# Merge stage of a hybrid encoder step: the mixed rows turned by VectorE instead of TensorE, two sets of product banks, the router one tile later

## The reference

```python
h = rmsnorm(x) * (1 + sc1) + sh1
o_hg, o_rw = hgrn2(h), rwkv7(h)                 # the two head groups: "mix", 1024 columns
x  = x + g1 * (concat(o_hg, o_rw) @ w_out)      # merge stage from here
h2 = rmsnorm(x) * (1 + sc2) + sh2
g_logits = h2 @ router_g_w + router_g_b         # 4 groups, top-1
e_logits = h2 @ router_e_w + router_e_b         # 8 experts in the group, top-2
gates = softmax(g_logits)[grp] * softmax(top2(e_logits))
x = x + g2 * sum(gates * expert(h2))            # 32 SwiGLU experts, then a final rmsnorm
```

## Time and profile before

| | us |
|---|---|
| median of 3 runs | 2940.0 (2937.04 to 2946.08) |
| the profiled execution's own time | 2939.38 |
| its span | 2937.6 |
| PE busy | 2701.2 (92%) |
| DVE busy | 1522.7 (52%) |
| ACT busy | 842.3 (29%) |
| merge products (L2184), first to last start | 1667.9 to 1954.9 |

### The profile page before, as it was taken

The page is one execution under the profiler, slowest core; times in us unless marked ns, Lnnn a source line. Parts: engine busy times, 40 slices in busy tenths (PEclk is TensorE's granted clock), DMA queues, the critical chain, the costliest instruction groups (busy, mean ns, idle before and its releaser), DMA issues. The chain is left out here.

```text
span 2937.6 us, 80216 instructions
## 1 busy us (share of the span) xinstructions
PE 2701.2 (92%) x33393; PEld 1697.0 (58%) x33394; DVE 1522.7 (52%) x3711; ACT 842.3 (29%) x1739; POOL 352.0 (12%) x477
## 2 busy tenths in 40 slices
PE   6998999999999979899998699976999999999978
PEld 2443445454454558778877455535666666666653
DVE  3554466665566647677777344454333333333328
ACT  2654334444344424444444222210000000000006
POOL 0000000000000001112113000001222222122223
PEclk8999999999999989999999799987999999999999
DMA  8433123223242396556652685572798578778758
GB/s 311 157 129 134 55 101 129 101 92 108 83 159 103 118 239 166 163 146 171 183 157 87 196 311 205 208 272 103 274 367 319 226 273 325 276 293 314 301 206 345
DMA packets 307724, 580.30 MB, mean 198 GB/s; under 512 B 56494, under 2 KB 240742, under 8 KB 292168
## 3 DMA queue, kind: packets, MB, share of 16 engines
q1 hardware_dynamic: 257544, 486.12, 46.8%
q0 software_dynamic: 18736, 70.27, 6.9%
q10 hardware_dynamic: 31248, 21.08, 2.4%
HBM read 411.77 MB, written 165.60 MB: 197 GB/s over the span
## 5 line engine op out<-in xcount | busy, mean ns | idle before, releaser
L555 PE MATMUL pj_P<-normed,pj_wc 128*128 128x448 f32 (+2 forms) x1600 | 593.6, 518 | 1.0 <-ACT pj_stage L279 1.0
L2751 PE MATMUL moe_PG<-wgu,moe_xT 128*32 128x256 f32 x9600 | 552.2, 381 | 41.3 <-DVE moe_hid L2605 24.3
L2751 PEld LDWEIGHTS moe_PG<-wgu,moe_xT 128*32 128x32 f32 x9600 | 372.2, 110 | 202.3 <-issue 64.5
L555 PEld LDWEIGHTS pj_P<-normed,pj_wc 128*128 128x128 f32 x1600 | 295.3, 190 | 259.0 <-issue 241.5
L2762 PE MATMUL moe_PTY<-wd,moe_hT 128*32 128x256 f32 x4800 | 291.1, 379 | 5.4 <-DVE moe_hT L2608 5.4
L2650 ACT ACTIVATE moe_sg<-moe_PG 128x128 f32<-128x128 f32 x150 | 41.7, 278 | 828.7 <-PE moe_PG L2751 652.5
L2591 DVE STREAM_TRANSPOSE moe_xT<-moe_xg 128x256 f32<-128x256 f32 x151 | 98.5, 653 | 320.5 <-PE moe_PG L2751 314.0
L2184 PE MATMUL merge_PO<-merge_w,merge_mT 128*128 128x512 f32 x544 | 238.7, 597 | 0.2 <-DMA merge_w<-in_w_out 0.2
L2762 PEld LDWEIGHTS moe_PTY<-wd,moe_hT 128*32 128x32 f32 x4800 | 187.3, 110 | 79.4 <-DVE moe_hT L2608 9.3
L2690 POOL DMA_INDIRECT moe_xg<-scratch_h,moe_row x152 | 148.6, 977 | 566.9 <-DVE moe_xT L2591 558.6
L2184 PEld LDWEIGHTS merge_PO<-merge_w,merge_mT 128*128 128x128 f32 x544 | 102.3, 191 | 123.7 <-issue 123.1
(11 more groups left out here) (431 smaller groups left out, 4009.2 us busy)
## 6 DMA issues: line engine op xcount, KB each, us to landing
wgu<-in_w_gate SPq DMA_DIRECT2D x32, 2048.0 KB
wgu<-in_w_up SPq DMA_DIRECT2D x32, 2048.0 KB
wd<-in_w_down SPq DMA_DIRECT2D x32, 2048.0 KB
scratch_y_rows<-merge_zeros SPq DMA_DIRECT2D x51, 512.0 KB, 4.7
scratch_hk<-pj_hk SPq DMA_DIRECT2D x16, 1344.0 KB, 5.1
normed<-scratch_hk SPq DMA_DIRECT2D x32, 640.0 KB, 8.0
re_hkf<-scratch_hk SPq DMA_DIRECT2D x32, 640.0 KB
scratch_y_rows<-moe_y ACTq DMA_DIRECT2D x604, 32.0 KB
```

The source lines that it names most:

```text
L555: ins = eng.matmul(bank[:, 0:wp], wc[:, j, k, :], hT[:, k, k0:k0 + wp], start=(k == 0), stop=(k == KD - 1), skip_group_check=True)
L2751: ins = eng.matmul(PG[32 * q:32 * q + 32, 0, 0:256].rearrange("p (a b) -> p a b", a=2), xT[:, k, :], wgu[p][:, :, k, 128 * q:128 * q + 128 ...
```

## The change

The mixed rows of a tile are loaded by four DMAs instead of one. DMA q fills partitions 32q to 32q + 31: partition 32q + t holds, for each of the four groups g of 32 tokens, columns 256q to 256q + 255 of token 32g + t. One VectorE transpose (32 x 32 squares) then writes the turned rows mT directly, in which partition p and block k hold channel 8p + k; w_out is loaded in the matching order, rows `(p k)` instead of `(k p)`. PE's `turn_m`, the banks PT0 and ACT's `keep_m` are gone. `turn_m` stands on DVE, in `norm`, between the sum x1 (L2301) and the 128 x 1 step (L2303), for tile n + 2. The free banks are a second PO, so tiles alternate between two. PE's body becomes out(n), logits(n - 2), turn_h(n - 1); ACT's exponentials and DVE's route are those of tile n - 2. Four tiles instead of two stand ahead of the loop. Behind the last tile PE does logits(15), turn_h(16), logits(16), ACT exponentials(15), keep_h(16), exponentials(16), and DVE route(15), route(16).

```diff
-        m_in = sb("m_in", [128, 2, D])
+        m_in = sb("m_in", [128, 2, 4, 256])
-        PT0 = ... psum_tensor("merge_PT0", [128, KD, 128], F32)
-        PO = ... psum_tensor("merge_PO", [128, 2, 512], F32)
+        PO = [... psum_tensor(f"merge_PO{p}", [128, 2, 512], F32) for p in range(2)]
-        LOOP = (NT - 5) // 2
+        LOOP = (NT - 7) // 2
@@ load_m (SP)
-                eng.dma_start(m_in[:, n % 2, :], t["mix"][ds(at_tile(i, n), 128), :]).then_inc(ev(f"m_in{n % 2}"), 16)
+                src = t["mix"][ds(at_tile(i, n), 128), :].rearrange("(g t) c -> t g c", g=4)
+                for q in range(4):
+                    eng.dma_start(m_in[32 * q:32 * q + 32, n % 2, :, :], src[:, :, 256 * q:256 * q + 256]).then_inc(ev(f"m_in{n % 2}"), 16)
@@ w_out (SP)
-  eng.dma_start(w[:, k, c], t["w_out"][0].rearrange("(k p) n -> p k n", p=128)[:, k, c])
+  eng.dma_start(w[:, k, c], t["w_out"][0].rearrange("(p k) n -> p k n", p=128)[:, k, c])
@@ tensor: turn_m removed
             def out(i, n):
-                eng.wait_ge(ev("mT_kept"), at(i, 4, 2 * n + 2))
-                if n:
-                    eng.wait_ge(ev("out_read"), at(i, 2, n))
+                eng.wait_ge(ev("m_turned"), at(i, 2, n + 1))
+                if n >= 2:
+                    eng.wait_ge(ev("out_read"), at(i, 2, n - 1))
             def body(i, n):
                 out(i, n)
+                if n >= 2:
+                    logits(i, n - 2)
                 if n:
                     turn_h(i, n - 1)
-                if not (i is None and n + 2 > NT - 1):
-                    turn_m(i, n + 2)
-                if n:
-                    logits(i, n - 1)
@@ scalar: keep_m removed
-                if n:
-                    exponentials(i, n - 1)
+                if n >= 2:
+                    exponentials(i, n - 2)
             tiles(eng, body)
+            exponentials(None, NT - 2)
             keep_h(None, NT - 1)
@@ vector
+            def turn_m(i, n):
+                eng.wait_ge(ev(f"m_in{n % 2}"), at(i, 64, 64 * (n // 2 + 1)))
+                eng.transpose(mT[:, n % 2, :, :].rearrange("p k (g t) -> p g k t", g=4),
+                              m_in[:, n % 2, :, :].rearrange("p g (c k) -> p g k c", k=KD)).then_inc(ev("m_turned"), 1)
                 eng.tensor_tensor(x1[:, p, :], x1[:, p, :], x[:, p, :], ALU.add).then_inc(ev("x1_ready"), 1)
+                if not (i is None and n + 2 > NT - 1):
+                    turn_m(i, n + 2)
             def body(i, n):
                 norm(i, n)
-                if n:
-                    route(i, n - 1)
+                if n >= 2:
+                    route(i, n - 2)
+            turn_m(None, 0)
+            turn_m(None, 1)
             tiles(eng, body)
+            route(None, NT - 2)
             route(None, NT - 1)
```

More of the change, by code:

```diff
@@ L2081, in merge @@
         zeros = sb("zeros", [128, D])
-        PT0 = ctx.enter_context(nc.psum_tensor("merge_PT0", [128, KD, 128], F32))
         PT1 = ctx.enter_context(nc.psum_tensor("merge_PT1", [128, KD, 128], F32))
-        PO = ctx.enter_context(nc.psum_tensor("merge_PO", [128, 2, 512], F32))
+        PO = [ctx.enter_context(nc.psum_tensor(f"merge_PO{p}", [128, 2, 512], F32)) for p in range(2)]
         PR = ctx.enter_context(nc.psum_tensor("merge_PR", [128, 512], F32))
         block = ctx.enter_context(nc.Block())
-        LOOP = (NT - 5) // 2
+        LOOP = (NT - 7) // 2
         def tiles(eng, body):
-            body(None, 0)
-            body(None, 1)
+            for n in range(4):
+                body(None, n)
             with eng.Fori(0, LOOP) as i:
-                body(i, 2)
-                body(i, 3)
-            for n in range(2 * LOOP + 2, NT):
+                body(i, 4)
+                body(i, 5)
+            for n in range(2 * LOOP + 4, NT):
                 body(None, n)
@@ L2148, in _ @@
                     k, c = slice(4 * part, 4 * part + 4), slice(512 * half, 512 * half + 512)
-                    eng.dma_start(w[:, k, c], t["w_out"][0].rearrange("(k p) n -> p k n", p=128)[:, k, c]).then_inc(ev(f"w_in{half}{part}"), 16)
+                    eng.dma_start(w[:, k, c], t["w_out"][0].rearrange("(p k) n -> p k n", p=128)[:, k, c]).then_inc(ev(f"w_in{half}{part}"), 16)
             load_x(None, 0)
@@ L2183, in out @@
                             eng.wait_ge(ev(f"w_in{half}{k // 4}"), 16)
-                        ins = eng.matmul(PO[:, half, :], mT[:, n % 2, k, :], w[:, k, 512 * half:512 * half + 512],
+                        ins = eng.matmul(PO[n % 2][:, half, :], mT[:, n % 2, k, :], w[:, k, 512 * half:512 * half + 512],
                                          start=(k == 0), stop=(k == KD - 1))
@@ L2209, in body @@
                 out(i, n)
+                if n >= 2:
+                    logits(i, n - 2)
                 if n:
                     turn_h(i, n - 1)
-                if not (i is None and n + 2 > NT - 1):
-                    turn_m(i, n + 2)
-                if n:
-                    logits(i, n - 1)
-            turn_m(None, 0)
-            turn_m(None, 1)
             tiles(eng, body)
+            logits(None, NT - 2)
             turn_h(None, NT - 1)
@@ L2224, in _ @@
         def _(eng):
[L2225 to L2230, removed]
             def keep_h(i, n):
@@ L2246, in body @@
                     keep_h(i, n - 1)
-                if not (i is None and n + 2 > NT - 1):
-                    keep_m(i, n + 2)
                 eng.wait_ge(ev("x1_ready"), at(i, 2, n + 1))
@@ L2297, in norm @@
                     eng.wait_ge(ev(f"x1_out{p}"), at(i, 16, 16 * (n // 2)))
-                eng.tensor_tensor(x1[:, p, :], PO[:, :, :].rearrange("p a b -> p (a b)"), m[:, 0, :], ALU.mult).then_inc(ev("out_read"), 1)
+                eng.tensor_tensor(x1[:, p, :], PO[p][:, :, :].rearrange("p a b -> p (a b)"), m[:, 0, :], ALU.mult).then_inc(ev("out_read"), 1)
                 eng.wait_ge(ev("out_read"), at(i, 2, n + 1))
```

8 lines of the change are left out of this document (removed).

## The result

The changed kernel takes 2909.96 us (median of four runs, 2903.41 to 2911.01) where the kernel before takes 2940.76 (four runs, 2937.04 to 2946.08): a ratio of 0.9888 [0.987, 0.9905]. The forecast was 2923.5 in a range of 2918 to 2932. So the sign is right, the gain (30.8 us) is nearly twice the 16.5 that was forecast, and the time lies outside the range.

What follows compares the result with a forecast made beforehand. PE was taken to set the merge stage's pace. The gap's -23.4, start's +2.5 and +1.0, and end's +4.1 summed to -15.8 us from 2939.4, giving 2923.5 us, range 2918 to 2932.

Steps and rivals of the forecast that it cites:

- a loss outside the stage: Outside the merge stage: a possible slowdown, given no size, counted within the 0.07 chance of a slower kernel.
- The gap between outs: PE, merge stage: gap from 3.33 to 1.93 us, period 15.77, saving 23.4 us from end of out(0) to end of out(16).
- The second PO: PE's product banks in the merge stage: removes the wait for out_read, credited with neither gain nor loss.
- The turn on DVE: DVE in norm: the 128x1024 transpose takes 2.1 us, 3.9 us stay spare, price on the path 0.
- Rival B: Merge stage: DVE binds through a long transpose; gain under 8.8 us from 6.6 us, 2952 at 8 us; 9%, 5 slower.
- The loads: Merge-stage m_in loads: four quarters take 1.35 us more per tile, hidden in steady state, cost to PE 0.
- rival C: Merge-stage m_in loads: a quarter takes as long as the whole did, 5.2 us a tile, giving 2932 us; 13%.
- m_in(5): Full DMA stretch near tile 3: lands at 1739.0, DVE waits some 5.9 us, PE loses 0.
- The start: Merge-stage start: +2.5 us for w_out behind more load issues and +1.0 for the clock, together +3.5.
- The clock: PE at out(0): slow piece of 3.9 us instead of 1.8 without preceding transposes, +1.0, bounds 0 and +2.
- The end: Merge-stage tail: three routes behind the last out, DVE done 20.7 us after it instead of 16.6, +4.1.

Runs made afterwards that it cites:

- b_u4: Kernel before with four tiles instead of two ahead of the merge stage's hardware loop; 2929.5 us, ratio 0.9953.
- b_tail328: Kernel before with 328 increments of an unused semaphore at the end of PE's list, behind the experts' last matmul; 2969.9 us, ratio 1.0095.
- turn_only: Changed kernel with logits, exponentials and route one tile earlier again, the turn staying on DVE; 2927.0 us, ratio 0.9945, period 17.12.
- route_only: Kernel before with four tiles ahead of the loop and logits, exponentials and route one tile later, turn_m staying on PE; 2924.8 us, ratio 0.9942, period 16.63.
- pad_act: Kernel before with 24 increments of an unused semaphore ahead of ACT's merge-stage work; 2940.5 us, ratio 1.0004.
- pad_sp: Kernel before with 14 increments of an unused semaphore at the end of SP's merge-stage list; 2942.7 us, ratio 1.0018.
- pad_dve: Kernel before with 60 increments of an unused semaphore ahead of DVE's merge-stage work; 2941.3 us, ratio 1.0015.
- b_s1024: Kernel before with eight tiles ahead of the loop and 40 increments of an unused semaphore in PE's list; 2938.1 us, ratio 0.999.
- pad_pe: Kernel before with 328 increments of an unused semaphore ahead of PE's merge-stage work; 2974.8 us, ratio 1.0123.
- b_s512: Kernel before with four tiles ahead of the loop and 184 increments of an unused semaphore ahead of PE's merge-stage list; 2955.3 us, ratio 1.0045.
- b_p72: Kernel before with 72 increments of an unused semaphore ahead of PE's merge-stage list; 2935.9 us, ratio 0.9994.
- a_u6: Changed kernel with six tiles instead of four ahead of the loop; 2914.3 us, ratio 0.9889.
- a_s512: Changed kernel with six tiles ahead of the loop and 42 increments of an unused semaphore ahead of PE's list; 2912.9 us, ratio 0.9886.
- a_u8: Changed kernel with eight tiles instead of four ahead of the loop; 2916.3 us, ratio 0.9916.

## Why the prediction was wrong, step by step

The failed step is the first sentence: "The diff touches one stage, so I read that stage and leave the rest as it is." By that the sum was taken from the execution's own time without a term for the 964 us behind the stage: that part was put at nothing without a reason, and the chances name only "a loss outside the stage", within the 0.07 for slower. In its place the runs showed a stage behind that is 14.6 us shorter, for which a term of about -13 was missing: b_u4, which computes and orders everything as before, has it (964.3 to 951.2 and a ratio of 0.9953 [0.9932, 0.9973]), and b_tail328 has 12.0 of it in the blocks, from instructions that run when the blocks are over. No row of the kernel before shows such a term; it could only be had from a run.

The steps of the stage itself held, -16.7 for a forecast of -15.8, closer than its terms were: 0.7 us too much for the gap and 1.7 too much for the start partly cancel.

- **The gap between outs**: a period of 15.77 forecast, 15.82 measured; from T(0) to T(16) 249.9 us instead of 272.6, 22.7 saved where 23.4 was forecast (14 periods, each 0.05 longer). turn_only and route_only show that the reason was right too. The second PO was given nothing, and nothing in these runs separates it.
- **The turn on DVE**: 2.1 forecast, 2.03 measured; it joins the line through 412 and 653 ns. Rival B is out: DVE is not the bound. By the rule of the Trainium skill (page "VectorE: DVE Perf Modes", section "Rules for kernel authors") the transposes should have stayed on TensorE and the sum been nought. turn_only agrees with it as far as the move alone brings nothing; route_only against after shows that with the later logits it is worth 16.63 - 15.82 = 0.81 us a tile.
- **The loads**: in the last seven tiles each quarter lands 3.0 to 4.2 us after its own issue, where the single load took 4.2 to 4.6. But the four issues are spread over 1.7 us, so the whole tile is there 4.9 to 5.9 us after the first, 0.3 to 1.7 later than before. The four loads are thus a little slower and hidden, both as forecast; what rival C wanted, 5.2 us for the bytes of a tile at the start, is not seen (below). In the full stretch m_in(5) landed 18.1 to 19.7 us after its issues, not 12.6, at about 1741 (1739.0 forecast), and DVE waited 7.1 us for it (5.9 forecast) without a gap on PE, as forecast.
- **The start**: +1.8 instead of +3.5. out(0) began 9.8 us after the stage's first load, where it had been 9.0: 0.8 of the 2.5 forecast. w_out's first quarter was issued 4.0 us after that load instead of 1.2, but landed 5.6 us after its issue instead of 7.7, so most of the issue times were hidden by bytes in flight and the lower bound of 0.7 was the right value. The clock: the granted clock is 0.50 (1.2 GHz) from 1665 to 1670, when PE did nothing, and 0.73 from 1670 to 1680, so it rose to 2.4 GHz at about 1675.4, after PE had streamed for 4.0 us from 1671.38; I had let out(0) have 3.9 us at the low level. It took 15.8 us (15.84 forecast).
- **The end**: DVE is done at T(16) + 20.9 (20.7 forecast), with three routes behind the last out.

**At like length** (b_u4 and after, +426 and +300, have blocks of 814.0 and 812.9) the change is worth about what the stage shows: b_u4 to after is 2929.5 to 2910.0, 19.5 us, of which 17.0 in the merge stage. By ratio 0.9888 / 0.9953 = 0.9935 (an estimate without an interval).

**What stays open.** How the length of the lists comes to act on the experts stage. Of the 9.5 us of idle time that went ahead of the gate and up products, 8.3 had ended with DVE's moe_hid (24.3 before, 16.0 after). Summed over the blocks, what they take above their floor of 5.18 us (the same in both kernels) falls from 55.8 to 41.2 us, and it is spread over many of the 150 blocks. DVE's waits for y's stores are 145.4 before and 145.7, 143.5, 141.6 and 143.7 in pad_act, pad_sp, pad_dve and b_s1024, against 130.1 after and 130.2, 133.1, 132.0 and 129.3 in b_u4, pad_pe, b_tail328 and b_s512. But they are as short (131.3 to 135.1) in b_p72, a_u6, a_s512 and a_u8, whose blocks take 5 to 8 us more than those of after, so they don't follow the blocks one to one. Transfers landing sooner, for instance because a longer program puts buffers at other addresses, would fit; no run moved a buffer alone, so this is only argued. A rival can be set aside: that the engines' lists are read again during the blocks. The queue that the profile calls "instruction" (q8) moved only 6 packets between 2010 and 2840 us in before, and 6 in b_tail328 and b_u4. Nor is it told apart whether PE's list counts or the sum of all lists: the pads on other engines were at most 60 long, and there are few points between +72 and +298.

## What to carry to other kernels

A wait and the work that hides it have to be removed together: the transposes alone gave 0, the later logits 0.5 a tile, both 1.3. Before a change is credited with a gain outside its stage, run the old schedule with the new one's length of code, and put padding behind everything as well as ahead of it; b_tail328 refuted in one run the reading that pad_pe had suggested and b_s1024 seemed to confirm. And when an edit moves the last tiles, read the waits in the tail first: the one that cost nothing there cost 5.64 us as soon as an out stood behind it.

## What was unexpected of the hardware

- The length of the instruction lists moves an untouched stage: 328 instructions appended at the very end take its blocks from 827.4 to 815.4 us, 0.4% of the kernel's time. In b_u4 the same effect gives a ratio of 0.9953 [0.9932, 0.9973] for the whole kernel, a gain without any change of the work.
- An idle increment costs PE some 0.15 us: with 72, 184 and 328 of them (b_p72, b_s512, pad_pe) PE's idle time ahead of the first transpose is 24.39, 42.18 and 63.75 us. At the end of the list they cost 0.13 us each (42.7 us for 328 in b_tail328). So PE's list is not free to lengthen.
- Splitting a load into four of 32 partitions each cost little: the whole tile landed 4.9 to 5.9 us after the first issue, where one load of 128 partitions took 4.2 to 4.6. The Trainium skill, page "SBUF — State Buffer", section "Door 1: The DMA port swizzle", has a transfer of 32 partitions reach half the ports. What the tile lost (0.3 to 1.7 us) is no more than the 1.7 us over which its four issues are spread, so the runs show no loss by ports beside it, and don't exclude one either.
